# First block of a three-block transformer kernel rebuilt: head norms by tables of statistics, modulation summed by VectorE, projections between the attention's heads

## The reference, cut to what matters

```python
mod = silu(c) @ w_ada + b_ada                       # 1024 -> 6144, one row
sh1, sc1, g1, sh2, sc2, g2 = split(mod, 6)
h = rms_norm(x, g_mix) * (1 + sc1) + sh1
q_lat, kv_lat, k_pe, qd, kd, vd = split(h @ w_in, ...)      # 512, 256, 32, 512, 512, 512
q  = rms_norm(q_lat) @ w_q_b                        # 8 heads x (64 + 32)
kv = rms_norm(kv_lat) @ w_kv_b                      # 8 heads x (64 + 64): k part and v
# every head: rms_norm of its 64 (or 32) columns with a gain, rope on the 32 (or the dilated 64)
o_mla = causal_attention(q, k, v)                   # 8 heads
o_dil = dilated_attention(qd, kd, vd)               # 8 heads, three window patterns
x = x + g1 * (concat(o_mla, o_dil) @ w_o)
h2 = rms_norm(x) * (1 + sc2) + sh2                  # then a gated feed-forward, "c"
```

## Time and profile before

| | |
|---|---|
| median of 3 runs | 2976.22 us (2970.95 to 2977.02) |
| the profiled execution | 2969.51 us, span 2967.8 us |
| TensorE busy | 2781.1 us |
| VectorE, ScalarE, GpSimd busy | 1285.1, 959.0, 302.4 us |
| mean granted clock of TensorE | 0.947 |

### The profile page before, as it was taken

One profiled execution on the slowest core, in us unless ns is written; L12 is line 12 of the kernel. 1 busy time (PEld: TensorE's weight loads), 2 busy tenths in 40 slices (PEclk: granted clock), 3 DMA queues, 4 the chain that ended last, 5 costly groups with the idle time before them and its releaser, 6 DMA issues.

```text
span 2967.8 us, 27881 instructions
## 1 busy us (share of the span) xinstructions
PE 2781.1 (94%) x11844; PEld 2212.0 (75%) x11844; DVE 1285.1 (43%) x1593; ACT 959.0 (32%) x1203; POOL 302.4 (10%) x191
## 2 busy tenths in 40 slices
PE   8869799989999999999779999999999987999997
PEld 7626566768888888887557888888888855788886
DVE  2666333255554433333555334343333446543333
ACT  2413233244332322222453222232222235432221
POOL 0134400000000011001110111001110021011100
PEclk9979777889999999999889999999999988999998
DMA  4202222222222222223102222232223321122221
GB/s 192 85 14 71 71 86 80 95 76 99 100 100 100 100 99 100 99 100 114 57 29 87 98 99 100 99 101 98 99 100 101 114 75 37 62 95 100 99 100 71
DMA packets 39245, 267.31 MB, mean 90 GB/s; under 512 B 5193, under 2 KB 5321, under 8 KB 8146
## 3 DMA queue, kind: packets, MB, share of 16 engines
q1 hardware_dynamic: 35280, 254.82, 24.9%
q0 software_dynamic: 2352, 6.32, 0.6%
q10 hardware_dynamic: 1490, 4.40, 0.4%
HBM read 263.40 MB, written 4.21 MB: 90 GB/s over the span
## 4 chain that ended last, share of the span: by engine, by line
PE 86%; DVE 5%; ACT 4%; issue 2%; POOL 2%; ACTq 0%; POOLq 0%; DVEq 0%
PE ps L315 25%; PE ps L316 25%; PE ps L317 25%; PE ps L457 2%; PE ps L492 2%; PE ps L343 2%; PE ps L447 1%; POOL wlo L1566 1%; ACT whi L719 1%; PE ps L482 1%; PE ps L601 1%; DVE sq L1441 1%; PE ps L630 1%; PE ps L622 1%; ACT PT L869 1%
## 5 line engine op out<-in xcount | busy, mean ns | idle before, releaser
L315 PE MATMUL ps<-ahi,whi 128*128 128x512 f32 x2328 | 932.3, 400 | 22.3 <-DVE alo L1123 19.4
L1082 DVE TENSOR_TENSOR wlo<-raw,whi 128x2048 fp32r<-128x2048 f32 x192 | 439.8, 2291 | 1143.0 <-ACT whi L719 1143.0
L316 PE MATMUL ps<-ahi,wlo 128*128 128x512 f32 x2328 | 915.2, 393 | 0.0
L317 PE MATMUL ps<-alo,whi 128*128 128x512 f32 x2328 | 914.4, 393 | 0.0
L719 ACT ACTIVATE whi<-raw 128x2048 fp32r<-128x2048 f32 x217 | 415.4, 1915 | 1030.6 <-PE ps L317 1030.6
L315 PEld LDWEIGHTS ps<-ahi,whi 128*128 128x128 f32 x2328 | 443.9, 191 | 130.2 <-issue 38.8
L316 PEld LDWEIGHTS ps<-ahi,wlo 128*128 128x128 f32 x2328 | 443.3, 190 | 98.5 <-issue 7.4
L317 PEld LDWEIGHTS ps<-alo,whi 128*128 128x128 f32 x2328 | 442.3, 190 | 94.3
L315 PE MATMUL ps<-hhi,whi 128*128 128x512 f32 x1024 | 408.2, 399 | 8.8 <-DVE hlo L1448 8.8
L316 PE MATMUL ps<-hhi,wlo 128*128 128x512 f32 x1024 | 403.4, 394 | 0.0
L317 PE MATMUL ps<-hlo,whi 128*128 128x512 f32 (+1 forms) x944 | 369.1, 391 | 0.0
(11 more groups left out here) (247 smaller groups left out, 1984.8 us busy)
## 6 DMA issues: line engine op xcount, KB each, us to landing
raw<-wstream SPq DMA_DIRECT2D x233, 1024.0 KB, 4.8
early<-ada_in SPq DMA_DIRECT2D x8, 1024.0 KB, 18.7
strip<-bias_strips POOLq DMA_DIRECT2D x16, 256.0 KB, 5.8
x<-x_in ACTq DMA_DIRECT2D x1, 2048.0 KB, 15.3
bias_strips<-bias_by_distance POOLq DMA_DIRECT2D x1, 2048.0 KB, 16.4
y_out<-x SPq DMA_DIRECT2D x4, 512.0 KB, 2.6
onehot<-bucket_in ACTq DMA_DIRECT2D x1, 640.0 KB, 3.9
bd<-lru_in ACTq DMA_DIRECT2D x2, 256.0 KB, 22.4
```

Source lines behind the costliest of these rows:

```text
L315: pe.matmul(out, wh, rhi, start=start, stop=False)
L316: pe.matmul(out, wl, rhi, start=False, stop=False)
L317: return pe.matmul(out, wh, rlo, start=False, stop=stop)
L1082: dve.tensor_tensor(wlo[s][:], raw[r][:], whi[s][:].bitcast(F32), ALU.subtract).then_inc(*inc("lo_dve", "lo", u))
```

## The change

The order of the first block is new, and so are three ways of computing in it. Head norms: the squares of each head are summed by a matmul with a selecting matrix (sel) into its own row of one table, 17 rows for q and k_pe, 10 for k, 16 for the dilated q and k; one root and one reciprocal serve a table, and a small product (scale) spreads a row over a tile, where VectorE multiplies (head). The rotation is done before the norm (turn, sine, rotate), with the gain inside the matrix and the cosine table. The root of a latent is folded into its table, v is scaled by it separately (values_ok). k and v of the kv unit are projected apart, k with 64 columns of weights. Modulation: blocks 1, 3, 5, 6, 7 and all 16 late ones are summed over the eight k tiles by VectorE (ada_acc) and over partitions by four one-column products (ada_sums). Order: the late blocks stand in the stream between the units; z tiles 0 to 7 are made in halves between the steps of heads 0 to 7 (z_half), 8 to 11 after them; w_o is taken in two parts, that of heads 0 to 7 (wo_part) between the steps of heads 8 to 15. All splits of the block are on VectorE, that of unit 1 behind the modulated tiles. The distance table and its way through DRAM come in the opening. PT has one buffer for two, and both masks share one. In the later layers only semaphores are merged. Cut to its core, indented less:

```diff
+ADA_AFTER = {("qb", 0): (8,), ("qb", 1): (9, 10), ("kvb", 0): (11, 12), ("z", 6): (13, 14), ("z", 8): (15, 16),
+     ("z", 10): (17, 18), ("z", 12): (19, 20), ("z", 14): (21,), ("z", 16): (22, 23)}
+BY_DVE = (1, 3, 5, 6, 7) + tuple(range(ADA_EARLY, U_ADA))
...
+    def ada_sums(a, b, lo):
...
+        pe.wait_ge(*at("ada_part", a, DT - 1))
+        part = acc[BY_DVE.index(a) % 2][:].rearrange("p (e n) -> p e n", e=2)
+        for m in range(2):
+            for e in range(2):
+                ins = pe.matmul(ps[:, b, lo + m:lo + m + 1], part[:, e, P * m:P * (m + 1)], C("ones")[:, 0:1],
+                                start=(e == 0), stop=(e == 1))
+        ins.then_inc(*inc("ada_mm", "ada_mm", a))
...
+    ada_columns(0)
...
+    ada_columns(2)
+    ada_sums(1, 7, 2)
+    for j in range(DT):
+        pe.wait_ge(*at("x_sq", "x", j))
+        pe.matmul(bank(3), C("ones"), sq[j % 2][:], start=(j == 0), stop=(j == DT - 1))\
+            .then_inc(*(inc("x_sum", "x_sum", j) if j < DT - 1 else inc("total", "total", "x")))
...
+    ada_columns(4)
+    ada_sums(3, 7, 6)
...
+    for a in (5, 6, 7):
+        ada_sums(a, 7, 2 * a)
...
+    def statistics(t):
...
+        n = NORMED.index(t)
...
+        elif t[0] == "k":
+            w = SEL_K + 10 - t[1]
+            ins = pe.matmul(ps[0:10, 2, :], sel[0:64, w:w + 10], sq[n % 2][0:64, :], start=False, stop=(t[1] == 7))
...
+    def turn(t):
...
+        elif t[0] == "q":
+            pe.wait_ge(*(at("sin", before(TURNED, t, 2)) if n >= 2 else at("lat_lo", "q", 3)))
+        b = 6 if t[0] == "z" else 6 + n % 2
+        pe.matmul(bank(b, rows), turn_by[by][0:rows, 0:rows], tile, start=True, stop=True).then_inc(*inc("turned_t", "turned_t", t))
...
+    def scale(t, b, *free):
...
+        elif t[0] == "k":
+            pe.wait_ge(*at("r", "kv"))
+            ins = pe.matmul(bank(b, 64), rows[0:10, 64 * t[1]:64 * t[1] + 64], r_kv[0:10, :], start=True, stop=True)
...
+    product("pe")
...
+    for n, t in enumerate(PROJECTED):
+        if n + 1 < len(PROJECTED):
+            product(PROJECTED[n + 1])
+        if t in TURNED:
+            turn(t)
+        if t in NORMED:
+            statistics(t)
+        if t in SUMS_AFTER:
+            pe.wait_ge(*at(*ada_before))
+            ada_sums(SUMS_AFTER[t], 1, 0)
+            ada_before = ("mod", SUMS_AFTER[t])
+    scale("pe", 0, ("rows",), ("lat_lo", "kv", 0))
+    scale(("q", 0), 1, ada_before)
+    scale(("q", 1), 0, ("head", "pe"))
+    for h in range(2, 8):
+        scale(("q", h), (h + 1) % 2, ("head", ("q", h - 2)))
+    scale("rms", 1, ("head", ("q", 6)))
+    scale(("k", 0), 3)
...
-    def ada_late(a):
...
-        for m in range(2):
-            for kt in range(DT):
-                ins = pe.matmul(ps[:, 6, 256 + m:257 + m], raw[AT["ada", a] % 2][:, kt * 2 + m, :], SILU_C[:, kt:kt + 1],
-                                start=(kt == 0), stop=(kt == DT - 1))
...
+    head_scores(0, ("values_ok", 3), ("head", ("q", 7)))
+    head_values(0)
+    scale(("k", 1), 5, ("tile", ("v", 2)))
+    for h in range(2, 8):
+        scale(("k", h), 3 if h % 2 == 0 else 5, ("head", ("k", h - 2)))
+    for h in range(8):
+        z_half(h, 0, 6, ("sin", ("z", h - 1) if h else ("q", 7)))
+        pe.wait_ge(*at("top", h))
+        ada_sums(13 + h, 2, 256)
+        z_half(h, 1, 6)
+        if h < 7:
+            head_scores(h + 1, ("mod", 13 + h))
         head_turn(h)
         head_mix(h)
...
-    wide(4, N_WO, "x_wo", lambda kt: ("out_lo", 2 * kt + 1), a_parts)
+        turn(("z", h))
+        statistics(("z", h))
+        if h % 2 and h < 7:
+            head_values(h + 1)
...
+    z_half(8, 0, 6, ("sin", ("z", 7)))
+    pe.wait_ge(*at("mod", 20))
+    ada_sums(21, 2, 256)
+    z_half(8, 1, 6)
+    z_half(9, 0, 0)
+    z_half(9, 1, 0)
+    head_values(8)
+    scale(("z", 0), 7)
+    scale(("z", 4), 5, ("out_lo", 7))
+    z_half(10, 0, 6, ("tile", ("z", 8)))
+    z_half(10, 1, 6)
+    head_scores(8, ("tile", ("z", 9)), ("mod", 21))
+    scale(("z", 1), 7, ("head", ("z", 0)))
+    scale(("z", 5), 5, ("head", ("z", 4)))
+    z_half(11, 0, 6, ("tile", ("z", 10)))
+    z_half(11, 1, 6)
...
+    def wo_part(c):
...
+        pe.wait_ge(*at("lo", u))
+        pe.wait_ge(*(at("x_part", c - 1) if c else at("tile", ("z", 11))))
+        pe.wait_ge(*at("out_lo", 7))
+        for kt in range(4):
+            ins = mm3(bank(6), u % 2, wo_block(c, kt), P, mla_out[kt][0][:], mla_out[kt][1][:], kt == 0, kt == 3)
...
+    for h in range(8, HEADS):
+        wo_part(h - 8)
+        if h < 10:
+            pe.wait_ge(*at("top", h))
+            pe.wait_ge(*at("mod", 13 + h))
+            ada_sums(14 + h, 2, 256)
+        if h + 1 < HEADS:
+            head_scores(h + 1, ("mod", min(14 + h, 23)))
+        if h in (8, 9, 10, 11):
+            t = {8: 2, 9: 6, 10: 3, 11: 7}[h]
+            scale(("z", t), 7, ("head", ("z", {2: 1, 6: 2, 3: 6, 7: 3}[t])))
+        if h == HEADS - 1:
+            pe.wait_ge(*at("out_lo", 13))
+            for c in range(4):
+                wo_rest(c, (0, 1, 2), ("x_part", 7) if c == 3 else ("top", h))
+        head_turn(h)
+        head_mix(h, *([("head", ("z", 5))] if h == 8 else []))
+        if h % 2 and h + 1 < HEADS:
+            head_values(h + 1)
+    for c in range(4):
+        wo_rest(c, (3,), ("out_lo", HEADS - 1))
+    for c in range(4, 8):
+        wo_rest(c, range(4), {4: ("turned", HEADS - 1, 2), 5: ("turned", HEADS - 1, 1), 6: ("out_lo", HEADS - 1), 7: ("head", ("z", 7))}[c])
...
+    def squares(t, rows, b):
...
+        act.activation(sq[n % 2][0:rows, :], bank(b, rows), ACT.Square).then_inc(*inc("tile", "tile", t))
...
+    def ada_acc(a):
+        k = BY_DVE.index(a)
...
+        dve.wait_ge(*(at("early", a) if a < ADA_EARLY else at("raw", AT["ada", a])))
...
+        if k >= 2:
+            dve.wait_ge(*at("ada_mm", BY_DVE[k - 2]))
+        for kt in range(DT):
+            w = (early[:, a, 2 * kt:2 * kt + 2, :] if a < ADA_EARLY else raw[AT["ada", a] % 2][:, 2 * kt:2 * kt + 2, :])\
+                .rearrange("p b n -> p (b n)")
+            c, y = SILU_C[:, kt:kt + 1], part[:, kt % 2, :]
+            if kt < 2:
+                dve.tensor_scalar(y, w, c, None, ALU.mult).then_inc(*inc("ada_part", "ada_part", a, kt))
+            else:
+                dve.wait_ge(*at("ada_part", a, kt - 2))
+                dve.scalar_tensor_tensor(y, w, c, y, ALU.mult, ALU.add).then_inc(*inc("ada_part", "ada_part", a, kt))
...
+    def sine(t):
...
+        dve.wait_ge(*at("turned_t", t))
+        dve.wait_ge(*(at("roped", TURNED[n - 2]) if n >= 2 else at("table", 1)))
+        dve.tensor_tensor(tmp[n % 2][0:rows, :], bank(b, rows), sin[0:rows, :], ALU.mult).then_inc(*inc("sin", "sin", t))
...
+    def head_recip(kind, n, r):
+        dve.wait_ge(*at("head_root", kind))
+        dve.reciprocal(r[0:n, :], r[0:n, :]).then_inc(*inc("r", "r", kind))
...
+    def head(t, b):
...
+        dve.wait_ge(*at("scale", t))
+        if t[0] == "k":
+            dve.scalar_tensor_tensor(kt_[0:64, t[1], :], kt_[0:64, t[1], :], col("g_k")[0:64], bank(b, 64), ALU.mult, ALU.mult)\
+                .then_inc(*inc("head", "head", t))
...
-    def norm_recip(t):
-        rows = JOBS[JOB_OF[t]][3]
-        r = slots[job_slot(t)][0][0:rows, :]
-        dve.wait_ge(*at("norm_root", t))
-        dve.reciprocal(r, r).then_inc(*inc("norm_r", "norm_r", t))
...
     head_top(0)
-    head_prob(0)
-    for h in range(HEADS):
+    for h in range(1, 8):
+        head(("k", h), 3 if h % 2 == 0 else 5)
+    for h in range(8):
+        head_prob(h)
+        ada_acc(14 + h)
+        ada_out(13 + h, 2, 256)
+        if h % 2 == 0:
+            split(8 + h // 2)
+        if h < 7:
+            head_top(h + 1)
+        sine(("z", h))
+        head_out(h)
+    split(12)
+    head_recip("z", 16, r_z)
+    ada_out(21, 2, 256)
+    ada_acc(22)
+    head(("z", 0), 7)
+    head(("z", 4), 5)
+    ada_acc(23)
+    split(13)
+    head_top(8)
+    head(("z", 1), 7)
+    head(("z", 5), 5)
...
+    for h in range(8, HEADS):
+        if h == 8:
+            split(14)
+        head_prob(h)
+        x_wo(h - 8)
...
+            ada_out(14 + h, 2, 256)
         if h + 1 < HEADS:
             head_top(h + 1)
-        ada_out(ADA_EARLY + h)
-        if h + 1 < HEADS:
-            head_prob(h + 1)
...
+        if h in (8, 9, 10, 11):
...
-    clear("wo")
-    split(N_WO + 2)
-    residual(N_WO, "x_wo", lambda j: mod[:, 16 + j:17 + j], None, "wo", 0)
...
-    for c in range(1, 4):
-        split(N_WO + c + 2)
-        residual(N_WO + c, "x_wo", lambda j: mod[:, 16 + j:17 + j], None, "wo", 2 * c)
+    split(16)
+    for j in range(0, DT, 2):
+        x_wo(8 + j)
+        x_wo(9 + j)
+        add_square("wo", j)
+        add_square("wo", j + 1)
+        if j == 2:
+            split(17)
+    split(18)
...
-    split(4)
...
+    def rotate(t):
...
+        pool.wait_ge(*at("turned_t", t))
+        pool.wait_ge(*at("cosines", 0 if t[0] == "z" else 1))
```

(41 more changed lines are left out.)

927 lines of the change are left out of this document (500 added, 427 removed).

## The result

| | before | after |
|---|---|---|
| median of the runs, us | 2976.3 (2970.95 to 2977.02) | 2848.8 (2846.18 to 2851.34) |
| ratio, 95% interval | | 0.9575 (0.9559 to 0.9592) |
| span of the profiled execution, us | 2967.8 | 2849.6 |
| mean granted clock | 0.947 | 0.960 |

The forecast was 2880, the range 2835 to 2930. The direction was right; the gain was 127.5 us, not 96, and the time lies inside the range. The windows of the new kernel, columns as in the earlier trace rows, are cut at its own stage borders: projections, heads 0 to 7, what lies between, heads 8 to 15, end of w_o and tail, and the first 349 us of the feed-forward.

The account below looks back on a forecast made before the run. TensorE, busy 94% of the span, was taken as the bound. Opening 58, projections 135, attention 313 and tail 16 sum to 522 us against 617.7, 96 less, so 2880; range 2835 to 2930.

Parts of the forecast that it names:

- Opening 58: Stage before the first product: ends at 58 us, between 54 and 62, against 80, set by VectorE's order.
- Projections 135: From first product to first scores: 130 us plus 5 for the clock, 135, between 118 and 150.
- The q tiles: Eight tiles in the projections: 40 us on TensorE, up to 50 on VectorE with the lock; taken as 45.
- the lock: GpSimd rotations block VectorE's two-operand operations at the shared SBUF port: 2.9 us for each of 17, 49 at most.
- The serial piece: End of the projections: reciprocal 3.35 and four multiplications of v and one of k, 7 us.
- Heads 0 to 7, 17.3 each: Attention, first eight heads: TensorE's sum 15.9 and VectorE's chain 16.4 nearly tie; taken as 17.3, 138 for eight.
- The chain: Heads 0 to 7: scaling, block, sums, scores through output and scaling again, with about 2 of handing over, 16.4 us.
- Heads 8 to 15, 12 each and 8 more: Attention, last eight heads: 12 us each, 96, and 8 for 36 products inside the last head.
- Clock 0.95: Mean clock over the attention's 297 us at full clock: 0.95 makes 313 us, between 297 and 330.
- The rival of cold transposes: In 16 heads, transposes, mix and turn at half clock: at most 56 us, forecast 2895 to 2920; chance 0.10.
- Clock unchanged: Heads 0 to 15: clock stays at 0.72, 297 us become 412, 2979 in all; chance 0.07, unchanged or lower.
- VectorE's queue becomes the bound: Late block loads hold VectorE's queue: a head takes 21.8, gain 45, about 2930; chance 0.15.

Follow-up runs that it names:

- the opening run: New kernel with its opening reordered: root of x earlier, blocks 6 and 7 ahead of the reciprocal, first split ahead of the modulation; 2833.8 us.
- the run with w_o ahead: New kernel with eight w_o parts in one piece ahead of head 8's transposes, instead of one inside each of heads 8 to 15; 2843.9 us.
- the run with the reciprocal ahead: New kernel with one further unused whole-tile reciprocal on VectorE in each of heads 0 to 7, ahead of the modulation block; 2871.0 us.

## Why the prediction was right, and where its sizes were off

*Opening 58.* Right, by its own terms: root at 41.50, reciprocal 3.35, VectorE's order sets it. That TensorE's queue is almost as late was not seen, and only matters once VectorE is faster: in the opening run VectorE then waits 4.39 us for it.

*Projections 135.* Right in the sum (138.1) by luck: two errors cancel. The q tiles were put at 45 because VectorE would pace them; TensorE does, in 40 (108.4 to 148), and the earlier trace rows were read rightly for the lock but its price hides. The serial piece was put at 7 and full clock; it takes 9, from 187.5 to 196.5, at 0.50, and the scaling of q and k_pe before it is half at the low level: from 176.5 to 196.5 the clock is 0.60. Eight q multiplications stand ahead of the second reciprocal on VectorE, which ends at 190.9.

*Heads 0 to 7, 17.3 each.* This is the term that was mis-sized: 15.0. The chain was put at 16.4, its steps at 14.4 and "about 2" for handing over. In the trace the whole chain, from the scores at 250.97 to the end of the modulation at 264.99, takes 14.0: the steps follow each other or overlap, and the 2 us are not there. (Its scaling takes 2.3 and not 1.5, which the shorter transposes make up for.) The chain also lists the sums behind the block; but the sums that a head's scores need are of a block made one head earlier, as the diff says (the loop sums 13 + h, VectorE makes 14 + h). So it runs scaling, block, modulation, scores, and ends 0.7 to 0.85 us before TensorE. TensorE's own sum was 15.9 with 2.4 for transposes and their waits. These were read from a head at full clock with two waits, 0.41 and the 0.47 shown there; in the new kernel one of 0.31 is left, and they take 1.7. And above a near tie I added 0.9 that nothing asked for.

*Heads 8 to 15, 12 each and 8 more.* 9.4 to 10.8 from one head's scores to the next where the clock is 1.00 (399.8 to 440.2); again the transposes, and a rest of 2.2 that is smaller.

*Clock 0.95.* About right as a mean (0.93 from 196.5 to the last w_o product), wrong in kind, so the mean owes something to luck: not a little lost everywhere but 1.00 in most heads, 0.58 from 196.5 to 218 and 0.64 from 369 to 396. *The rival of cold transposes* falls: every head has ten of them, and in most the mix takes 2.37 at clock 1.00. The Trainium skill, TensorE: Matmul & The Clock Gate, Part 4, says that transposes do not count as busy; the run with w_o ahead, heads of scores, transposes and mix alone, shows at any rate that with 1.7 us of them in heads of 7.5 us the clock stays at 1.00. *Clock unchanged* falls as well. Its grounds, small fp32 products and waits, do go with the two low stretches, but those are 49 us of the 280. What the forecast set against it, that the single-column products are gone, was the right reason: put back, they cost 37 us by the clock alone.

*VectorE's queue becomes the bound.* Not as it stood; the run with the reciprocal ahead shows how near it was: some 0.8 us a head.

*Tail 16, transfers hidden, part behind 2350.* 15.1; TensorE never waits for a load in the heads; 2350 to 2357 in all traces.

## What to carry to other kernels

Take matrix-vector work off TensorE first: besides its own time it took the clock from what stood behind it in most heads here, and wide products beside it did not prevent that. Then look for each wait of some 2 us on TensorE and price it double, as those of 2.2 to 2.4 us cost here; the order of a few instructions on two engines (the split ahead of the modulation above all) was worth 8 to 12 us. And before adding up a chain over loops, look which turn of the loop makes what this turn reads, and take its handing over from a trace. A difference of a few microseconds in one trace can be the clock alone, as the next section shows.
